# Last two output columns of a decoder layer: their tokens split 384 + 136 instead of 256 + 264

## The chip, the cores and the metric

The kernel runs on one core of one Trainium2 chip. The metric is the device time of one execution in microseconds (us); lower is better. A core has TensorE (PE, matmuls; its weight loads are shown apart as PEld), VectorE (DVE), ScalarE (ACT), GpSimd (POOL) and SyncE (SP), which run their own instruction streams and wait for each other by semaphores, and 16 DMA engines. A queue issues a DMA from the instruction stream of SP or ACT.

## What is computed

One layer of a hybrid decoder on 512 prompt tokens and 8 sample tokens (520 together), model width 2048, all in f32:

```python
h = h + jnp.concatenate([o, pool_out], axis=-1) @ w_out
gate, up = jnp.split(rmsnorm(h, g_ffn) @ w_gate_up, 2, axis=-1)
h = h + (jax.nn.silu(gate) * up) @ w_down
h = h + jax.nn.sigmoid(rmsnorm(h, g_ple) @ w_ple_gate) * (p_i @ w_ple_proj)
...
y_prompt = rmsnorm(hp, g_final)
y_sample = rmsnorm(hs, g_final)
```

The change lies in the last two lines' stage: the gated per-layer embedding (the fourth line) and the final norm, whose result `y_prompt` (512 x 2048) is 4.2 MB and `y_sample` (8 x 2048) 64 KB.

## The kernel before

Activations are kept transposed: a tile is 128 model columns (partitions) by T = 520 tokens, and h is 16 such tiles (KD = 16, P = 128). Each f32 product is made of three matmuls in rounded f32 (`float32r`): weights and activations are split into a high and a low part, and high x high, high x low and low x high are summed in PSUM. ScalarE makes the high part of the weights (L1378), VectorE the low part (L1932). Every matmul has its own load of 128 x 128 weights.

In the last stage a column tile m of the output needs 16 x 3 matmuls over the model width for the gate (accumulator `acc`), and 2 x 3 for the projection of the embedding (`scores`). Then VectorE multiplies the gate's sum by the row's inverse root (`gate_row`), ScalarE takes the sigmoid, VectorE multiplies by the projection and adds to h, ScalarE writes h times the final gain (`hg_row`) and h squared, GpSimd adds up the squares over the tiles, TensorE turns the scaled tile into rows of tokens (one transposition for each block of 128 tokens, into `mail_bank`, and one for the 8 sample tokens, into `o_bank`), and ScalarE copies the rows back over h. In tiles 0 to 13 all 520 tokens go together, as two matmuls of 260 columns each.

The last two tiles, 14 and 15, are split by tokens, so that a part of the tokens is complete before the matmuls end. `quarter(i)` gives for i = 0 to 3 the tile (s = 0, 1), the part of the tokens (a = 0, 1), its slice and its length: quarters 0 and 1 are the first 256 tokens of tiles 14 and 15, quarters 2 and 3 the remaining 264. TensorE runs for each quarter `half_column` (24 matmuls), the turn of the quarter before (`half_turn`, L1331), 12 matmuls, for i = 2 and 3 the row sums of the squares (`row_sums`, L1342: a matmul of 128 x 128 squares with a column of ones for each block), the last 12 matmuls and six of the projection. A turn waits until ScalarE has written the scaled copy (`hg_ready`).

When the row sums of a part are there (`fin_stats`), `finish(a)` runs on ScalarE (L1902) and VectorE (L2605): ScalarE takes the roots (after a table load), VectorE the reciprocals, and then they scale the finished rows, 8 tiles (half of a block of 128 rows, 512 KB) at a time. ScalarE scales block 2a and stores each half itself (L1914, L1916); VectorE scales block 2a + 1 (L2615), and SP stores it when `y_scaled` says so (L706). The instructions of an engine run in the order of the code: on ScalarE and VectorE it is `half_column(0)`, `half_column(1)`, `finish(0)`, `half_column(2)`, `half_column(3)`, `finish(1)`. So the first half's stores are issued while TensorE works on quarters 2 and 3. The sample rows (`ys_nat`) are scaled and stored at the very end (L2617, L708). SP finally waits for all nine stores of y.

Of the kernel before, what the change touches and what calls it, by code (L numbers as in the profile page):

```python
# [20 lines left out]
ALU = mybir.AluOpType  # L21
ACT = mybir.ActivationFunctionType
# [6 lines left out]
P = 128  # L29
D = 2048  # L30
SEQ = 512
NB = 8
T = SEQ + NB
# [21 lines left out]
HK = KD // 2  # L55
# [158 lines left out]
def quarter(i):  # L214

    s, a = i % 2, i // 2
    return s, a, (slice(0, 2 * P), slice(2 * P, T))[a], (2 * P, T - 2 * P)[a]


def is_first(i):  # L220
# [9 lines left out]
def layer(nc, x_prompt, x_sample, p_prompt, p_sample, cache_k, cache_v, state_pool, page_table,  # L230
# [17 lines left out]
    with ExitStack() as ctx:  # L248
# [3 lines left out]
        def ps(name, shape):  # L252
            return ctx.enter_context(nc.psum_tensor(name, shape, F32))

        def sem(name):
            return ctx.enter_context(nc.semaphore(name))
# [42 lines left out]
        sum_sq = sums[:, 0:T]  # L299
        sq = [sums[:, (2 + i) * T:(3 + i) * T] for i in range(2)]  # L300
# [8 lines left out]
        h_all = late.rearrange("p (k t) -> p k t", k=KD)  # L309
# [65 lines left out]
        fin = region[:, 8 * T + D:8 * T + D + 16]  # L375
# [45 lines left out]
        acc = [ps(f"acc{i}", [P, 2, 512]) for i in range(2)]  # L421
        sc = ps("scores", [P, 2, 512])
        mbank = ps("mail_bank", [P, 512])
# [3 lines left out]
        def out(t):  # L427
            return acc[t % 2][:, :, 0:HT]

        fin_sums = [acc[0][:, 0, 320:321], acc[0][:, 0, 321:322], acc[1][:, 0, 320:321], sc[:, 0, 320:321],  # L430
                    acc[0][0:NB, 0, 322:323]]
        bank_x = [acc[0][:, 0, 0:HT], acc[1][:, 0, 0:HT]]
        bank_y = [acc[0][:, 1, 0:HT], acc[1][:, 1, 0:HT]]
        bank_z = [sc[:, 0, 0:HT], sc[:, 1, 0:HT]]
# [16 lines left out]
        S = {n: sem(n) for n in names}  # L451
# [12 lines left out]
        def y_rows(b, k):  # L464

            return y_prompt[0, b * P:(b + 1) * P, :].rearrange("p (k n) -> p k n", n=P)[:, k:k + HK, :]

        def y_cells(b, k):

            return h_all[:, k:k + HK, b * P:(b + 1) * P]  # L470
# [7 lines left out]
        def _(sp):  # L478
            def load(slab, src, first=False):

                if not first:
                    sp.wait_ge(S["w_low_done"], slab.index - 1)
                k = src.shape[1]
                sp.dma_start(raw[slab.slot][:, :].rearrange("p (k n) -> p k n", k=k), src)\
                    .then_inc(raw_landed[slab.slot], 16)
# [215 lines left out]
            load_wp(KD // 2 - 1)  # L701
            for m in (KD - 2, KD - 1):
                load(Slab(PLE_N + m), w_pg_v[:, :, m * P:(m + 1) * P])
            for n, (b, k) in enumerate(((1, 0), (1, HK), (3, 0), (3, HK))):
                sp.wait_ge(S["y_scaled"], n + 1)
                sp.dma_start(y_rows(b, k), y_cells(b, k)).then_inc(S["y_stored"], 16)  # L706
            sp.wait_ge(S["y_scaled"], 5)
# [8 lines left out]
        def _(pe):  # L716
# [11 lines left out]
            def begin(slab, t, first=False):  # L728
                pe.wait_ge(S["w_low_done"], slab.index + 1)
                if not first:  # L730
                    pe.wait_ge(S["acc_free"], t - 1)
# [599 lines left out]
            def half_turn(i):  # L1331

                s, a, tokens, n = quarter(i)
                pe.wait_ge(S["hg_ready"], KD - 2 + i + 1)
                pe.wait_ge(S["y_taken"], KD - 2 + i)
                for b in (2 * a, 2 * a + 1):
                    ins = pe.transpose(mbank[:, b * P:(b + 1) * P], hg_row[s][:, b * P:(b + 1) * P], ident)
                if a:
                    ins = pe.transpose(obank[0:NB, 0:P], hg_row[s][:, SEQ:T], ident)
                ins.then_inc(S["y_turned"], 1)  # L1340

            def row_sums(squares, blocks, start, stop):  # L1342

                def add(out, rows):
                    return pe.matmul(out, rows, ones[:, 0:1], start=start, stop=stop, skip_group_check=True)
                for b in blocks:
                    ins = add(fin_sums[b], squares[:, b * P:min((b + 1) * P, T)])
                return ins

            for i in range(4):  # L1350
                if i < 2:
                    begin(Slab(PLE_N + KD - 2 + i), PLE_T + KD - 2 + i)
                half_column(i, range(HK))
                if i == 0:
                    turn_y(KD - 3, 1)
                else:
                    half_turn(i - 1)
                half_column(i, range(HK, HK + 4))
                if i == 2:
                    pe.wait_ge(S["pool_summed"], KD * 2 + KD)  # L1360
                    row_sums(sum_sq, (0, 1), True, True).then_inc(S["fin_stats"], 1)
                elif i == 3:
                    pe.wait_ge(S["pool_summed"], KD * 2 + KD + 1)
                    row_sums(sum_sq, (2, 3, 4), True, False)
                half_column(i, range(HK + 4, KD)).then_inc(S["acc_ready"], 1)
                half_projection(i)
            half_turn(3)
            pe.wait_ge(S["squared"], KD * 2 + KD + 2)
            row_sums(sq[1], (2, 3, 4), False, True).then_inc(S["fin_stats"], 1)

        @block.scalar
        def _(act):
            A = Steps(act, S["act_step"])
# [50 lines left out]
            for k in range(KD):  # L1424
                c, b = divmod(k, 4)
# [453 lines left out]
            def half_column(i):  # L1879

                s, a, tokens, n = quarter(i)
                m, done = KD - 2 + s, KD - 2 + i + 1
                tile = h_all[:, m, tokens]
                act.wait_ge(S["acc_free"], PLE_T + done)
                act.activation(silu_row[s][:, tokens], gate_row[s][:, tokens], ACT.Sigmoid).then_inc(S["silued"], 1)
                if i == 3:
                    act.activation(fin[:, 7:8], eps, ACT.Sqrt, scale=1.0 / D, bias=eps)
                act.wait_ge(S["pool_summed"], KD * 2 + m - 1)
                act.wait_ge(S["h_done"], done)
                act.activation(hg_row[s][:, tokens], tile, ACT.Copy,  # L1890
                               scale=gains[:, m + V_FINAL:m + V_FINAL + 1]).then_inc(S["hg_ready"], 1)
                act.activation(sq[s][:, tokens], tile, ACT.Square).then_inc(S["squared"], 1)
                if i == 1:
                    act.activation(fin[:, 5:6], eps, ACT.Sqrt, scale=1.0 / D, bias=eps)
                act.wait_ge(S["squared"], KD * 2 + done)
                act.wait_ge(S["y_turned"], done)
                if a:
                    act.activation(ys_nat[:, m * P:(m + 1) * P], obank[0:NB, 0:P], ACT.Copy)
                act.activation(h_all[:, m, a * 2 * P:(a + 1) * 2 * P], mbank[:, a * 2 * P:(a + 1) * 2 * P],
                               ACT.Copy).then_inc(S["y_taken"], 1)  # L1900

            def finish(a):  # L1902

                act.wait_ge(S["fin_stats"], a + 1)
                for b in ((0, 1), (2, 3, 4))[a]:
                    n = NB if b == 4 else P
                    act.activation(fin[0:n, b:b + 1], fin_sums[b], ACT.Sqrt, scale=1.0 / D,
                                   bias=eps[0:n, :]).then_inc(S["fin_root"], 1)
                if not a:
                    act.activation(fin[:, 6:7], eps, ACT.Sigmoid)  # L1910
                act.wait_ge(S["fin_inv"], 2 * a + 1)
                act.wait_ge(S["y_taken"], KD + 2 * a)
                for k in (0, HK):
                    A.step(act.activation(y_cells(2 * a, k), y_cells(2 * a, k), ACT.Copy, scale=fin[:, 8 + 2 * a:9 + 2 * a]))  # L1914
                    A.wait()
                    act.dma_start(y_rows(2 * a, k), y_cells(2 * a, k)).then_inc(S["y_stored"], 16)  # L1916
            half_column(0)
            half_column(1)
            finish(0)
# [5 lines left out]
        def _(dve):  # L1925
            V = Steps(dve, S["dve_step"])
            tt, stt, ts = dve.tensor_tensor, dve.scalar_tensor_tensor, dve.tensor_scalar
# [615 lines left out]
            for v in range(ND):  # L2543
                n, q = NS + v, len(resident(v // 4)[1])
# [59 lines left out]

            def finish(a):  # L2605

                dve.wait_ge(S["fin_root"], 2 + 3 * a)
                dve.reciprocal(fin[:, 8 + 2 * a:10 + 2 * a], fin[:, 2 * a:2 * a + 2]).then_inc(S["fin_inv"], 1)
                if a:
                    dve.reciprocal(fin[0:NB, 12:13], fin[0:NB, 4:5]).then_inc(S["fin_inv"], 1)  # L2610
                dve.wait_ge(S["fin_inv"], 2 * a + 1)
                dve.wait_ge(S["y_taken"], KD + 2 * a)
                for k in (0, HK):
                    cells_b = y_cells(2 * a + 1, k)
                    ts(cells_b, cells_b, fin[:, 9 + 2 * a:10 + 2 * a], None, ALU.mult).then_inc(S["y_scaled"], 1)  # L2615
                if a:
                    ts(ys_nat, ys_nat, fin[0:NB, 12:13], None, ALU.mult).then_inc(S["y_scaled"], 1)  # L2617
            half_column(0)
# [72 lines left out]
```

## Time and profile before

| | us |
|---|---|
| median of 3 runs | 2339.3 (2337.1 to 2341.42) |
| the profiled execution, device time | 2344.21 |
| its span in the trace | 2342.4 |
| TensorE busy in the span | 2270.8 (97%) |
| VectorE busy | 1639.2 (70%) |
| ScalarE busy | 1080.8 (46%) |
| GpSimd busy | 191.8 (8%) |
| mean granted clock of TensorE | 0.99 |

The page of a profile shows how busy each engine was, 40 slices of the span, the DMA queues, the chain of work that ended last (followed back from the last instruction to whatever released it), and groups of instructions. Times on the trace's axis start at the span's begin; the split tiles lie between 2296.9 and its end. A busy TensorE isn't TensorE at its peak, and the trace gives matmuls a modelled end: the pace is read from the starts of many, as in the chain, and not from the mean of one. An engine's idle time costs only if it is on the chain.

### The profile page before, as it was taken

The numbers are of one execution on the slowest core, as the hardware profiler recorded it, in microseconds if no ns is written. First come the engines' busy times: TensorE is split into PE (matmuls) and PEld (weight loads), VectorE is DVE, ScalarE is ACT, GpSimd is POOL, SyncE is SP. The second block draws the span as 40 slices with busy tenths as digits, with TensorE's granted clock in tenths as the row PEclk, the third lists the DMA queues.
The fourth block names the chain that finished last, engine by engine and source line by source line (L and its number), as shares of the span: only waits on it lengthen the run. The fifth ranks groups of instructions, "written<-read, shape, count | busy, mean of one in ns | idle before, by whom it ended". The sixth has DMA issues, their size and how long they took to land.

```text
span 2342.4 us, 45807 instructions
## 1 busy us (share of the span) xinstructions
PE 2270.8 (97%) x18549; PEld 2219.8 (95%) x18549; DVE 1639.2 (70%) x2125; ACT 1080.8 (46%) x1639; POOL 191.8 (8%) x88
## 2 busy tenths in 40 slices
PE   7999999999999999999999999999899999989997
PEld 6988898888999999999999999999899999979997
DVE  5355555564257888888888888888777777885333
ACT  5334444443245455454445454554434444564434
POOL 0041112301221000000000000000000000121111
PEclk9999999999999999999999999999999999999999
DMA  7454565543334445454554545457966865532332
GB/s 251 141 167 155 163 195 179 175 122 128 93 90 150 119 134 171 139 171 139 161 149 136 160 132 161 136 171 224 299 178 191 235 179 148 148 90 82 88 107 80
DMA packets 488018, 359.44 MB, mean 153 GB/s; under 512 B 8417, under 2 KB 469298, under 8 KB 487001
## 3 DMA queue, kind: packets, MB, share of 16 engines
q1 hardware_dynamic: 474921, 347.31, 50.2%
q10 hardware_dynamic: 13000, 10.78, 1.4%
q8 instruction: 67, 1.10, 0.2%
q14 instruction: 30, 0.25, 0.0%
HBM read 301.23 MB, written 57.29 MB: 153 GB/s over the span
## 4 chain that ended last, share of the span: by engine, by line
PE 91%; DVE 4%; DMA 2%; ACT 2%; issue 1%; SPq 0%; ACTq 0%; DVEq 0%
PE acc L1161 39%; PE acc L718 30%; PE scores L1161 15%; PE scores L718 2%; PE mail_bank L718 1%; PE o_bank L718 1%; DMA x_low<-act_low_rows 1%; DVE w_low L2378 1%; DVE w_low L1932 1%; DMA region<-in_x_prompt 1%; PE mail_bank L882 0%; DVE raw L2382 0%; ACT w_high L1378 0%; DVE x_low L1940 0%; DMA raw<-in_w_ple_gate 0%
## 5 line engine op out<-in xcount | busy, mean ns | idle before, releaser
L1161 PE MATMUL acc<-x_high,w_high 128*128 128x260 f32 x1584 | 449.2, 284 | 9.0 <-DMA x_low<-act_low_rows 6.4
L718 PE MATMUL acc<-x_high,w_high 128*128 128x260 f32 (+2 forms) x2048 | 437.4, 291 | 11.0 <-DVE w_low L1932 6.3
L1161 PE MATMUL acc<-x_low,w_high 128*128 128x260 f32 x1584 | 448.0, 283 | 0.0
L1161 PE MATMUL acc<-x_high,w_low 128*128 128x260 f32 x1584 | 447.7, 283 | 0.0
L718 PE MATMUL acc<-x_high,w_low 128*128 128x260 f32 (+2 forms) x2048 | 421.8, 284 | 0.0
L718 PE MATMUL acc<-x_low,w_high 128*128 128x260 f32 (+2 forms) x2048 | 421.5, 284 | 0.0
L2378 DVE TENSOR_TENSOR w_low<-raw,w_high 128x1024 fp32r<-128x1024 f32 (+4 forms) x252 | 285.6, 1134 | 121.3 <-ACT w_high L1704 120.3
L718 PEld LDWEIGHTS acc<-x_high,w_high 128*128 128x128 f32 x2048 | 320.4, 190 | 33.8 <-issue 24.2
L2378 DVE TENSOR_TENSOR w_low<-key_pages,w_high 128x1024 fp32r<-128x1024 f32 (+4 forms) x252 | 283.5, 1132 | 89.0 <-ACT w_high L1704 88.0
L718 PEld LDWEIGHTS acc<-x_low,w_high 128*128 128x128 f32 x2048 | 321.0, 190 | 0.1
L718 PEld LDWEIGHTS acc<-x_high,w_low 128*128 128x128 f32 x2048 | 321.0, 190 | 0.0
L1704 ACT ACTIVATE w_high<-key_pages 128x1024 fp32r<-128x1024 f32 (+4 forms) x252 | 244.4, 984 | 142.3 <-PE acc L1161 62.7
L1161 PEld LDWEIGHTS acc<-x_high,w_high 128*128 128x128 f32 x1584 | 299.2, 189 | 10.2 <-issue 7.4
L1161 PE MATMUL acc<-half_sums_high,w_high 128*128 128x260 f32 x1056 | 300.2, 284 | 5.0 <-DVE w_low L2378 3.0
L1704 ACT ACTIVATE w_high<-raw 128x1024 fp32r<-128x1024 f32 (+4 forms) x252 | 244.5, 984 | 120.8 <-PE acc L1161 58.4
L1161 PEld LDWEIGHTS acc<-x_low,w_high 128*128 128x128 f32 x1584 | 299.7, 189 | 0.0
L1161 PEld LDWEIGHTS acc<-x_high,w_low 128*128 128x128 f32 x1584 | 299.6, 189 | 0.0
L1161 PE MATMUL acc<-half_sums_low,w_high 128*128 128x260 f32 x1056 | 299.4, 283 | 0.0
L1161 PE MATMUL acc<-half_sums_high,w_low 128*128 128x260 f32 x1056 | 298.8, 283 | 0.0
L1707 ACT ACTIVATE sums<-acc 128x260 f32<-128x260 f32 x216 | 83.1, 385 | 322.6 <-PE acc L1161 321.7
L1161 PEld LDWEIGHTS acc<-half_sums_high,w_high 128*128 128x128 f32 x1056 | 198.9, 188 | 6.8 <-DVE w_low L2378 3.8
L1161 PEld LDWEIGHTS acc<-half_sums_high,w_low 128*128 128x128 f32 x1056 | 199.7, 189 | 0.0
(313 smaller groups left out, 4015.9 us busy)
## 6 DMA issues: line engine op xcount, KB each, us to landing
raw<-in_w_gate_up SPq DMA_DIRECT2D x44, 1024.0 KB, 6.8
key_pages<-in_w_gate_up SPq DMA_DIRECT2D x44, 1024.0 KB, 7.6
raw<-in_w_in SPq DMA_DIRECT2D x32, 1024.0 KB, 7.1
act_high_rows<-late_rounded SPq DMA_DIRECT2D x22, 910.0 KB, 5.3
act_low_rows<-late_rounded SPq DMA_DIRECT2D x22, 910.0 KB, 7.0
key_pages<-in_cache_k SPq DMA_DIRECT2D x32, 512.0 KB, 5.9
late<-in_cache_v SPq DMA_DIRECT2D x32, 512.0 KB, 6.0
raw<-in_w_out SPq DMA_DIRECT2D x16, 1024.0 KB, 5.8
```

What stands on the lines that cost most here:

```text
L718: return pe.matmul(o, l, r, start=start, stop=stop)
L1161: return pe.matmul(bank, w, x, start=start and first, stop=last, skip_group_check=True)
L1704: act.activation(wh[PLACE[i] // 2][:, at:at + q * P], src[:, 0:q * P], ACT.Copy).then_inc(S["part_high"], 1)
L1707: act.activation(dest, src, ACT.Copy).then_inc(S["copied"], 1)
L1932: tt(wl[slab.home][:, 0:n * P], raw[slab.slot][:, 0:n * P], wh[slab.home][:, 0:n * P].bitcast(F32), ALU.subtract).then_inc(S["w_low_done"], 1)
L2378: tt(wl[PLACE[i] // 2][:, at:at + c], src[:, 0:c], wh[PLACE[i] // 2][:, at:at + c].bitcast(F32), ALU.subtract).then_inc(S["part_low"], 1)
```

## The change

The first part now has three blocks of tokens (384), the second one block and the sample tokens (136). Everything that counts blocks follows: the turns take 3 and 1 blocks (`PART_BLOCKS`), the row sums blocks 0 to 2 and then 3 and the samples; in the first `finish` ScalarE takes three roots and scales and stores three halves (both of block 0 and the first of block 2), VectorE three (both of block 1 and the second of block 2), and in the second `finish` each has one half of block 3. Row sums have other cells of PSUM. The number of matmuls over the model width and of stores is the same.

```diff
@@ quarter, L214 @@
-    return s, a, (slice(0, 2 * P), slice(2 * P, T))[a], (2 * P, T - 2 * P)[a]
+    return s, a, (slice(0, 3 * P), slice(3 * P, T))[a], (3 * P, T - 3 * P)[a]
+
+
+PART_BLOCKS = ((0, 1, 2), (3,))
@@ fin_sums, L430 @@
-        fin_sums = [acc[0][:, 0, 320:321], acc[0][:, 0, 321:322], acc[1][:, 0, 320:321], sc[:, 0, 320:321],
-                    acc[0][0:NB, 0, 322:323]]
+        fin_sums = [acc[0][:, 0, 400:401], acc[0][:, 0, 401:402], acc[0][:, 0, 402:403], sc[:, 0, 400:401],
+                    acc[1][0:NB, 0, 400:401]]
@@ sync, L704 @@
-            for n, (b, k) in enumerate(((1, 0), (1, HK), (3, 0), (3, HK))):
+            for n, (b, k) in enumerate(((1, 0), (1, HK), (2, HK), (3, HK))):
@@ tensor: half_turn and row sums @@
-                for b in (2 * a, 2 * a + 1):
+                for b in PART_BLOCKS[a]:
...
-                    row_sums(sum_sq, (0, 1), True, True).then_inc(S["fin_stats"], 1)
+                    row_sums(sum_sq, (0, 1, 2), True, True).then_inc(S["fin_stats"], 1)
...
-                    row_sums(sum_sq, (2, 3, 4), True, False)
+                    row_sums(sum_sq, (3, 4), True, False)
...
-            row_sums(sq[1], (2, 3, 4), False, True).then_inc(S["fin_stats"], 1)
+            row_sums(sq[1], (3, 4), False, True).then_inc(S["fin_stats"], 1)
@@ scalar: half_column and finish @@
-                act.activation(h_all[:, m, a * 2 * P:(a + 1) * 2 * P], mbank[:, a * 2 * P:(a + 1) * 2 * P],
-                               ACT.Copy).then_inc(S["y_taken"], 1)
+                rows = slice(a * 3 * P, SEQ if a else 3 * P)
+                act.activation(h_all[:, m, rows], mbank[:, rows], ACT.Copy).then_inc(S["y_taken"], 1)
...
-                for b in ((0, 1), (2, 3, 4))[a]:
+                for b in ((0, 1, 2), (3, 4))[a]:
...
-                for k in (0, HK):
-                    A.step(act.activation(y_cells(2 * a, k), y_cells(2 * a, k), ACT.Copy, scale=fin[:, 8 + 2 * a:9 + 2 * a]))
+                for b, k in (((0, 0), (0, HK), (2, 0)), ((3, 0),))[a]:
+                    A.step(act.activation(y_cells(b, k), y_cells(b, k), ACT.Copy, scale=fin[:, 8 + b:9 + b]))
                     A.wait()
-                    act.dma_start(y_rows(2 * a, k), y_cells(2 * a, k)).then_inc(S["y_stored"], 16)
+                    act.dma_start(y_rows(b, k), y_cells(b, k)).then_inc(S["y_stored"], 16)
@@ vector: finish @@
-                dve.wait_ge(S["fin_root"], 2 + 3 * a)
-                dve.reciprocal(fin[:, 8 + 2 * a:10 + 2 * a], fin[:, 2 * a:2 * a + 2]).then_inc(S["fin_inv"], 1)
+                dve.wait_ge(S["fin_root"], 3 + 2 * a)
+                blocks = slice(3, 4) if a else slice(0, 3)
+                dve.reciprocal(fin[:, 8:12][:, blocks], fin[:, 0:4][:, blocks]).then_inc(S["fin_inv"], 1)
...
-                for k in (0, HK):
-                    cells_b = y_cells(2 * a + 1, k)
-                    ts(cells_b, cells_b, fin[:, 9 + 2 * a:10 + 2 * a], None, ALU.mult).then_inc(S["y_scaled"], 1)
+                for b, k in (((1, 0), (1, HK), (2, HK)), ((3, HK),))[a]:
+                    ts(y_cells(b, k), y_cells(b, k), fin[:, 8 + b:9 + b], None, ALU.mult).then_inc(S["y_scaled"], 1)
```

The instructions of ScalarE from the row sums of the first part to quarter 2 (L1907 is a root, L1914 a scaling, L1916 its store, L1885 the sigmoid of a quarter), before:

```order
L1907 ACTIVATE region<-acc,constants 128x1 x2
L1910 ACT_TABLE_LOAD
L1910 ACTIVATE region<-constants 128x1
L1914 ACTIVATE late<-late,region 128x8x128
L1916 DMA out<-late 128x8x128
L1914 ACTIVATE late<-late,region 128x8x128
L1916 DMA out<-late 128x8x128
L1885 ACTIVATE region<-region 128x264
```

and after, with lines numbered three higher:

```order
L1910 ACTIVATE region<-acc,constants 128x1 x3
L1913 ACT_TABLE_LOAD
L1913 ACTIVATE region<-constants 128x1
L1917 ACTIVATE late<-late,region 128x8x128
L1919 DMA out<-late 128x8x128
L1917 ACTIVATE late<-late,region 128x8x128
L1919 DMA out<-late 128x8x128
L1917 ACTIVATE late<-late,region 128x8x128
L1919 DMA out<-late 128x8x128
L1888 ACTIVATE region<-region 128x136
```

One scaling and one store more stand ahead of the sigmoid of quarter 2. The same engine at the end of the program, from the last copies of turned rows on (L1898, L1899; then the roots, for which `scores` and `acc` hold the row sums), before:

```order
L1898 ACTIVATE region<-o_bank 8x128
L1899 ACTIVATE late<-mail_bank 128x256
L1907 ACTIVATE region<-acc,constants 128x1
L1907 ACTIVATE region<-scores,constants 128x1
L1907 ACTIVATE region<-acc,constants 8x1
L1914 ACTIVATE late<-late,region 128x8x128
L1916 DMA out<-late 128x8x128
L1914 ACTIVATE late<-late,region 128x8x128
L1916 DMA out<-late 128x8x128
```

and after:

```order
L1901 ACTIVATE region<-o_bank 8x128
L1903 ACTIVATE late<-mail_bank 128x128
L1910 ACTIVATE region<-scores,constants 128x1
L1910 ACTIVATE region<-acc,constants 8x1
L1917 ACTIVATE late<-late,region 128x8x128
L1919 DMA out<-late 128x8x128
```

One root, one scaling and one store are gone there. TensorE in the middle of quarter 3, around the turn of quarter 2 (L1337, L1339) that waits for ScalarE's scaled copy, before:

```order
L718 MATMUL acc<-x_low,w_high 128x264
L718 MATMUL acc<-x_high,w_low 128x264
L1337 MATMUL mail_bank<-constants,region 128x128 x2
L1339 MATMUL o_bank<-constants,region 8x128
L718 MATMUL acc<-x_high,w_high 128x264
```

and after:

```order
L721 MATMUL acc<-x_low,w_high 128x136
L721 MATMUL acc<-x_high,w_low 128x136
L1340 MATMUL mail_bank<-constants,region 128x128
L1342 MATMUL o_bank<-constants,region 8x128
L721 MATMUL acc<-x_high,w_high 128x136
```

The order is the same; a turn has one block instead of two, and the matmuls around it have 136 columns instead of 264.

## Rows read from the trace of the kernel before

**Rows 1.** The page, the chain that ended last: shares of the span by engine.

```profile
PE 91%; DVE 4%; DMA 2%; ACT 2%; issue 1%; SPq 0%; ACTq 0%; DVEq 0%
```

**Rows 2.** The chain from 2296 us on: start us, us, what, how many.

```profile
2296.89 2.84 PE acc L718 x24
...
2310.41 2.91 PE acc L718 x24
2313.32 0.22 PE mail_bank L1337 x2
...
2314.99 0.35 PE acc L1345 x4
...
2315.79 1.28 ACT L1910
...
2320.44 0.43 ACT region L1885
...
2322.53 0.44 PE mail_bank L1337 x2
...
2326.68 0.44 DVE region L2598
...
2331.54 1.16 ACT late L1914
```

**Rows 3.** ScalarE's timeline of the first finish; last, TensorE's waits, total, times, longest.

```profile
2317.20 1.14 ACT L1914 ACTIVATE late<-late,region 128x1024 f32<-128x1024 f32 x1
...
2318.81 1.15 ACT L1914 ACTIVATE late<-late,region 128x1024 f32<-128x1024 f32 x1 [0.48 <-ACT late L1914]
...
2320.44 0.42 ACT L1885 ACTIVATE region<-region 128x264 f32<-128x264 f32 x1 [0.48 <-ACT late L1914]
...
PE mail_bank L1337 <- ACT region L1890: 4.3, 2, 2.3
```

**Rows 4.** Weight loads by shape: busy us, mean ns of one; last, timeline of four loads.

```profile
L718 PEld LDWEIGHTS acc<-x_high,w_low 128*128 128x128 f32 x2048 | 321.0, 190 | 0.0
...
L1345 PEld LDWEIGHTS acc<-constants,sums 128*128 128x128 f32 x8 | 1.1, 189 | 0.1
...
L1289 PEld LDWEIGHTS o_bank<-constants,region 128*8 128x8 f32 x14 | 1.2, 87 | 0.0
...
2314.71 0.53 PEld L1345 LDWEIGHTS acc<-constants,sums 128*128 128x128 f32 x4
```

**Rows 5.** Matmuls by shape, plain f32 of few columns: busy us, mean ns of one.

```profile
L718 PE MATMUL mail_bank<-constants,late 128*128 128x2 f32 x128 | 14.7, 246 | 0.0
...
L718 PE MATMUL o_bank<-v_nat,small 128*128 128x128 f32 x96 | 14.1, 283 | 0.0
```

**Rows 6.** Operations of 520 and 264 columns, grouped by shape: busy us, mean ns.

```profile
L1859 ACT ACTIVATE region<-region 128x520 f32<-128x520 f32 x1 | 0.6, 637 | 5.6 <-DVE region L2579 5.6
...
L2598 DVE TENSOR_TENSOR region<-acc,rstd 128x264 f32<-128x264 f32 x2 | 0.9, 430 | 4.8 <-PE acc L718 4.8
...
L2579 DVE TENSOR_TENSOR region<-acc,rstd 128x520 f32<-128x520 f32 x1 | 0.7, 699 | 8.0 <-PE acc L718 8.0
```

**Rows 7.** Windows: engines' busy us (instructions), then granted clock, DMA share, GB/s.

```profile
156.00:160.00 4.00, 0.42 (x4) 0.21 (x2) 3.97 (x6) 0.00 (x0) 0.92 (x1) 1.00 0.41 128
...
161.00:164.00 3.00, 3.00 (x16) 3.00 (x15) 0.79 (x3) 1.29 (x6) 0.74 (x1) 0.50 0.93 343
...
553.00:557.00 4.00, 0.97 (x6) 0.75 (x4) 0.69 (x5) 3.58 (x12) 0.00 (x0) 1.00 0.01 2
557.00:563.00 6.00, 5.31 (x17) 4.53 (x18) 3.02 (x6) 2.32 (x6) 0.00 (x0) 0.50 0.84 313
...
2322.00:2324.00 2.00, 1.47 (x13) 1.45 (x14) 0.00 (x0) 1.32 (x4) 0.75 (x1) 1.00 1.04 302
```

**Rows 8.** DMA from 2330 to 2343 us: rate in 40 slices of 0.325 us, sum.

```profile
GB/s 0 0 0 0 0 0 0 0 0 8 265 254 328 230 323 298 301 295 238 326 299 299 301 304 302 298 414 203 175 184 274 233 173 175 136 19 0 0 0 0
DMA packets 4176, 2.16 MB, mean 166 GB/s; under 512 B 72, under 2 KB 4168, under 8 KB 4168
```

## The prediction

> **What bounds the kernel now.** I read the chain that ended last first: 91% of the span is TensorE [rows 1], so every microsecond of matmul counts until the stage's own end. Then the same chain over the last 47 us, where the whole change lies [rows 2]. The reader is to see four stretches there. Up to 2315.36 the chain is TensorE alone: quarter 0 of the split (column tile 14, tokens 0 to 255) begins at 2296.89 and takes 24 matmuls in 2.84 us for each half of its K sum, 0.118 us a matmul; quarters with 264 tokens take 2.91 us for 24, 0.121 us. From 2315.36 to 2322.53 it is ScalarE: the first `finish` (roots, a table load of 1.28 us, two scalings and two stores), after which comes the sigmoid of quarter 2, and only then what TensorE needs for `half_turn(2)`. TensorE runs out of work at about 2320.7 and stands still; its two waits for ScalarE's L1890 add up to 4.3 us, the other of them is at the very end [rows 3]. From 2322.53 to 2326.68 it is TensorE again, and from there to 2331.54 the chain of short operations that ends in the last scalings. From 2331.54 to the span's end at 2342.4, 10.86 us, the program scales and stores 2.16 MB [rows 8].
>
> **Wide quarters.** Quarters 0 and 1 grow from 256 to 384 tokens. No row has a rounded-f32 matmul of 384 columns; the step from 256 to 264 columns costs 0.003 us for 8 [rows 2], 0.41 ns a column, which is 2.4 GHz. So 384 columns take 0.118 + 128 x 0.00041 = 0.171 us. Each quarter has 48 + 6 matmuls: 108 x 0.0533 = **+5.8 us**, all on the path. Each turn gets a third block, 0.11 us each [rows 2]: +0.2 us. Slabs, low parts and the `acc_free` waits are ready long before; these cost nothing.
>
> **Narrow quarters.** Here is where I choose. If 136 columns cost what the slope says, a matmul takes 0.121 - 128 x 0.00041 = 0.069 us, and the wide quarters' loss is given back. But every matmul has its own load of 128 x 128 weights. A load of 8 columns lasts 87 ns and one of 128 lasts 190 ns, for rounded and plain f32 alike: 103 ns for 120 columns [rows 4]. The row sums, whose matmuls have one column and can't hold anything up, show loads spaced (0.53 - 0.19)/3 = 0.113 us [rows 4], and 128 matmuls of two columns kept TensorE busy 14.7 us, 0.115 us each [rows 5]. Those are plain f32, but the load is the same row. I take **0.114 us**: almost nothing is gained by making a matmul narrower than about 245 columns. The bounds are 0.069 us (the slope) and 0.147 us (a plain f32 matmul of 128 columns [rows 5]); 0.114 is nearest to the rows that have the same load.
>
> **To the first sums.** Quarter 2 has 36 matmuls ahead of its row sums: 36 x (0.114 - 0.121) = -0.25 us. The row sums take three blocks for two, two more records of 0.09 us: +0.2 us. They also wait for the squares of quarter 1. Before, the chain passes from the matmuls to the sums with no wait between [rows 2], and the two operations each on ScalarE and VectorE that lead to the squares grow by some 0.5 us at the slopes of [rows 3, 6]; GpSimd's addition grows too, by an amount that I don't know. TensorE gets there 0.15 us earlier after quarter 1's accumulator, with its six projection matmuls 0.3 us longer. I count 0, with +1 us as the bound. Sum at `fin_stats`: 5.8 + 0.2 - 0.25 + 0.2 = **+5.9 us** (2321.3 on the old axis).
>
> **ScalarE's first finish.** It now scales and stores three half blocks for two. One scaling and its store take 2318.81 - 2317.20 = 1.61 us [rows 3]; a third root takes 0.15 us. Queued behind on the same engine is quarter 2's sigmoid, on that VectorE's product, ScalarE's scaled copy, and `half_turn(2)` on TensorE. All of it is on the path: **+1.8 us**. VectorE's three scalings (0.7 us each) end long before the sigmoid. The pieces after the sigmoid are narrower. ScalarE gains (0.637 - 0.422)/256 = 0.84 ns a column, VectorE (0.699 - 0.430)/256 = 1.05 ns [rows 3, 6]; two operations on each with 128 columns fewer give -0.5 us. TensorE resumes at 2322.53 + 5.9 + 1.8 - 0.5 = 2329.7, +7.2 us. It ran out of work 42 narrow matmuls after the sums, 42 x 0.114 = 4.8 us, at 2326.1: the stall grows from 1.8 to **3.6 us**.
>
> **From the resumption to the last scalings.** One block fewer to turn (-0.11), 24 matmuls at -0.007 (-0.16), two records of row sums fewer (-0.2): -0.45 us. Then, up to the scalings, gate, sigmoid and scaled copy are narrower (-0.35), one block fewer is turned and copied (-0.2), one root fewer (-0.15): -0.7 us; VectorE's product and sum lie under the table load there and give nothing. The last scalings begin 7.2 - 0.45 - 0.7 = **+6.05 us** later.
>
> **The stores at the end.** Only block 3 and the sample rows are left, 1.11 MB for 2.16. At full rate the engines moved about 300 GB/s and at the end some 180 [rows 8]; the last part, with the sample rows, stays. 1.05 MB at 300 GB/s are 3.5 us, at the mean of 260 GB/s 4.0. I take **-3.7 us**. Issue doesn't bound it: ScalarE's last store leaves 1.6 us earlier after the scalings than before, with 0.5 MB still to move. The early stores, 3.1 MB, are issued up to 2328.1 and done by about 2335.5, ahead of the last ones (2338.3 and later).
>
> Sum at full clock: 6.05 - 3.7 = **+2.3 us**.
>
> **The clock.** The longer stall has a price of its own. TensorE's granted clock stayed at 1.00 through the present stall of 1.8 us [rows 7]. It fell to 0.50 (1.2 of 2.4 GHz) around both stalls of 3.6 us or so that the rows show: TensorE did nothing from 156.4 to 160.0, and from 161 to 164 it ran at 0.50; it stood from 554 to 557.7, and 557 to 563 are at 0.50 [rows 7]. The stage after the stall is 3.6 us of matmuls. With 3 us of them at half clock, if the loads slow down with it, some 1.5 us are lost, and a transposition or two more cost 0.1 each: **+1.6 us** (bounds 0 and 3.3, the whole stage at half clock). I take the fall as likelier than not, since a stall of this length never went by without one.
>
> Forecast: +3.9 us. The profiled execution would go from 2344.2 to 2348.1; the median of the runs, 2339.3, is 4.9 us below the profiled one, and I add to that: **2343.2 us**, 0.17% above. About 0.2%, 4.7 us, is the least that a measurement of this kernel tells from no change, so this is within it, and close to its edge.
>
> **Rivals.**
> (a) The clock holds through the stall: +2.3 us, 2341.6. For it: the stall of 1.8 us left it alone; against it: both of the longer ones.
> (b) Narrow matmuls follow their columns, 0.069 us. Then the sums are ready at most 0.6 us sooner than in my sum, since ScalarE's table load and copy of quarter 1 bound `finish` there; the stall ends by ScalarE as before; the last 24 give 24 x 0.045 = 1.1 us: +0.6 us at full clock, +1.6 with a fall, about 2340.4. For it speaks the slope of [rows 2], against it the spacing of the loads in [rows 4]. The Trainium skill, TensorE: Matmul & The Clock Gate, Back-to-back issue gap, gives columns divided by 2.4 GHz plus 2.5 ns for an isolated warm matmul, an estimate of 59 ns for 136 columns, which would come to this rival; no row here shows so narrow a matmul with a full load at that pace.
> (c) Slower: a rounded-f32 matmul this narrow loses its rate and costs what plain f32 does. One record at 0.15 us adds 36 x 0.036 = 1.3 us before the sums and 24 x 0.036 = 0.9 at the end: +6.1 us with the clock's fall, 2345.4. As two records of 0.147 us (0.29), TensorE and no longer ScalarE bounds the stretch after the sums: 6.3 + 3.9 + 4.2 more, +16.7 us, 2356. It decides from about 0.155 us a matmul even with the clock held. For it: the trace has no rounded matmul under 256 columns; against it: load and duration are otherwise alike.
> (d) The last stores are bound by latency rather than bytes, and 1.05 MB fewer save only 2 us: +5.6 us, 2344.9. Against it: the rate is near 300 GB/s for most of [rows 8].
> (e) The change does what it is meant to and more, since ScalarE's longer hold is hidden (the stores' issue overlapping the table load or the like) and the clock holds: -5 us or better. No row shows an 8 us error in my sum.
>
> **Chances.** Forecast 0.48 (its range 2341 to 2345.5); (a) 0.17, (b) 0.12, (c) 0.10, (d) 0.09, (e) 0.04. Slower by over 0.2% takes most of (c) and (d), and a third of the forecast's own case, which its bounds carry over the edge: 0.33. Faster: 0.05. Same: 0.62. The range reaches from (b) less the scatter of the runs to (c) in its milder form and the clock's upper bound: 2339.2 to 2348.
>
> **What would show each step.** 24 matmuls of quarter 0 in 4.1 us, and of quarter 2 in 2.75 us (1.65 under (b), 3.6 or more under (c)); the first `finish` on ScalarE 1.6 us longer, with three stores; TensorE's longest wait for L1893's copy some 3.6 us; a granted clock of 0.50 in the 3 us around the last 24 matmuls; 1.11 MB after the last scalings. I am wrong if the narrow matmuls are not near 0.114 us, or if the part after the last scaling shrinks by less than 3 or more than 4.5 us.

## The result

| | kernel before | changed kernel |
|---|---|---|
| median of 11 runs each, us | 2341.5 (2337.1 to 2346.1) | 2347.3 (2342.3 to 2348.5) |
| ratio, with its 95% interval | | 1.0023 (1.0016 to 1.0031) |
| span of the profiled execution, us | 2342.4 | 2343.5 |
| start of the first split matmul on its axis, us | 2296.9 | 2291.7 |
| from there to the end of the span, us | 45.5 | 51.85 |

By the ratio the changed kernel is slower by 0.23%, 5.4 us (3.7 to 7.3). The spans of the two profiled executions differ by 1.1 us only, since in the second the work ahead of the split tiles, which is the same program, happened to end 5.2 us earlier. So I compare from the start of the first split matmul: **the stage takes 6.3 us more**, and that agrees with the ratio. Every later figure "after the stage's start" is counted that way. A second profiled execution of the changed kernel (c_after, below) gave a span of 2346.8 us and a stage of 51.9.

The chain of the changed kernel, from the page:

```profile
PE 90%; DVE 5%; DMA 2%; ACT 2%; issue 1%; SPq 0%; ACTq 0%; DVEq 0%
```

Its end, the same view as [rows 2] (start us, us, what, how many; the lines of the changed kernel are numbered three higher):

```profile
2291.65 4.21 PE acc L721 x24
...
2311.46 2.63 PE acc L721 x24
2314.09 0.35 PE mail_bank L1340 x3
...
2315.74 0.62 PE acc L1348 x6
...
2322.79 1.11 ACTq L1919
...
2323.94 0.33 ACT region L1888
...
2325.55 0.47 PE mail_bank L1340
...
2326.24 2.46 PE acc L721 x12
...
2331.93 0.31 DVE region L2601
...
2336.32 0.75 DVE late L2618
```

A wide quarter takes 4.21 us for 24 matmuls, 0.175 us each, a narrow one 2.63 us, 0.110 us. The first root begins at 2316.38, 24.73 us after the stage's start against 18.47 before. TensorE resumes at 2325.55. Twelve matmuls that took 1.29 us before the stall take 2.46 us after it.

ScalarE's hold, the same view as [rows 3] (DMA_DIRECT2D is the issue of a store; the last line is TensorE's wait: total, times, longest):

```profile
2321.61 1.15 ACT L1917 ACTIVATE late<-late,region 128x1024 f32<-128x1024 f32 x1 [0.48 <-ACT late L1917]
2322.79 1.11 ACTq L1919 DMA_DIRECT2D out<-late  x1
2323.94 0.32 ACT L1888 ACTIVATE region<-region 128x136 f32<-128x136 f32 x1 [1.19 <-issue]
...
PE mail_bank L1340 <- ACT region L1893: 5.8, 2, 4.5
```

The third store's issue took 1.11 us where the first two took 0.40. TensorE stands still 4.5 us, from 2321.05 to 2325.55; in the kernel before it was 2.0 us (4.3 in two waits, less the one of 2.3 at the end [rows 3]).

The clock and the last stores, the same views as [rows 7] and [rows 8] (windows as there; rate in 40 slices of 0.35 us from 2330 us on, and its sum):

```profile
2316.00:2320.00 4.00, 4.00 (x38) 4.00 (x38) 2.46 (x5) 3.11 (x7) 0.00 (x0) 1.00 0.27 81
2326.00:2332.00 6.00, 6.00 (x32) 5.96 (x30) 0.07 (x1) 0.42 (x2) 0.25 (x1) 0.50 0.63 182
...
GB/s 0 0 0 0 0 0 0 0 0 0 0 0 0 0 0 0 0 0 0 0 0 0 16 268 278 322 301 299 299 303 301 306 389 103 0 0 0 0 0 0
DMA packets 2096, 1.11 MB, mean 80 GB/s; under 512 B 40, under 2 KB 2088, under 8 KB 2088
```

TensorE begins 38 groups of matmuls in 4 us at 1.00 and only 32 in 6 us at 0.50. The granted clock fell during the stall, at 2323.6, 2.6 us after TensorE had stopped. It wasn't back at 2333.2, after 7.6 us of work without a gap, nor later. The stores at the end do what they should: 1.11 MB instead of 2.16, and none of the slow tail of [rows 8].

Where the 6.3 us come from, in times after the stage's start:

| us | before | changed | difference |
|---|---|---|---|
| first root of the first finish | 18.47 | 24.73 | +6.26 |
| from it to the sigmoid of quarter 2 | 5.08 | 7.56 | +2.48 |
| from that until TensorE resumes | 2.09 | 1.61 | -0.48 |
| from there to quarter 3's gate | 4.15 | 6.38 | +2.23 |
| from there to the last scalings | 4.86 | 4.39 | -0.47 |
| from there to the end of the span | 10.86 | 7.18 | -3.68 |
| sum | 45.51 | 51.85 | +6.34 |

### The profile page after: what moved, and what is told of

The parts are those of the page before. It is cut to its first block, busy times and chain, and to the rows that moved or that the text cites. A ratio compares the mean times of both kernels' runs of the same rounds, so it can differ in the third digit from the quotient of the medians.

```text
span 2343.5 us, 45803 instructions
## 1 busy us (share of the span) xinstructions
PE 2277.2 (97%) x18547; PEld 2226.7 (95%) x18547; DVE 1637.8 (70%) x2125; ACT 1081.1 (46%) x1639; POOL 191.7 (8%) x88
## 4 chain that ended last, share of the span: by engine, by line
PE 90%; DVE 5%; DMA 2%; ACT 2%; issue 1%; SPq 0%; ACTq 0%; DVEq 0%
PE acc L1164 39%; PE acc L721 30%; PE scores L1164 15%; PE scores L721 2%; PE mail_bank L721 1%; PE o_bank L721 1%; DVE w_low L2381 1%; DMA x_low<-act_low_rows 1%; DVE w_low L1935 1%; DMA region<-in_x_prompt 1%; DVE x_low L1943 1%; PE mail_bank L885 0%; DVE raw L2385 0%; ACT w_high L1381 0%; DMA raw<-in_w_down 0%
```

## The experiments

The stage's time is one trace for each version; the two traces of the changed kernel agree within 0.03 us (51.85 and 51.88). Each ratio is to the kernel before in the same set of runs; where the intervals of two versions overlap, only the traces tell them apart. Of each edit the lines that carry it are shown.

My theory after this result: the split itself costs 6.3 us of TensorE, since a matmul can't be spaced closer than its weight load; ScalarE's hold makes a stall of 4.5 us; that stall costs half of the clock for the rest of the stage, some 3 us; and the stores give 3.7 us back. The main rivals: the clock falls because the matmuls are narrow, whatever the stall; or all of the loss is stall and clock and the split costs nothing.

**e1_act_two: the hold back to two stores.** ScalarE takes two halves, VectorE four:

```diff
-                for b, k in (((0, 0), (0, HK), (2, 0)), ((3, 0),))[a]:
+                for b, k in (((0, 0), (0, HK)), ((3, 0),))[a]:
...
-                for b, k in (((1, 0), (1, HK), (2, HK)), ((3, HK),))[a]:
+                for b, k in (((1, 0), (1, HK), (2, 0), (2, HK)), ((3, HK),))[a]:
```

> The changed kernel, but ScalarE scales and stores two halves in the first finish and VectorE four (SP stores those). Theory (ScalarE's third scaling and its store of 1.11 us hold back quarter 2, and the stall that follows costs the clock): ScalarE reaches the sigmoid of quarter 2 about 5.1 us after its first root instead of 7.6, TensorE stands still 2.0 us instead of 4.5, the clock stays at 1.00, and the stage from the first split matmul to the span's end (51.85 us changed, 45.5 before) takes about 46.3 us. Rival (the clock falls because the matmuls are narrow, whatever the stall): the stall is 2 us, but the matmuls after it are spaced 0.213 us, and the stage takes about 49.4 us. Rival (the third store of a queue is slow only with ScalarE's): SP's third and fourth stores are issued in 0.4 us each; if it goes by the queue they take about 1.0.

Measured: the sigmoid 5.24 us after the first root, a longest wait of 2.1 us, the stage 48.64 us for the 46.3 of the theory; ratio to the kernel before 1.0014 (1.0005 to 1.0024). So the hold was on the path: 2.3 us went with it. But the clock fell all the same, a microsecond after TensorE resumed at 2326.0 (windows; and, last, SP's third and fourth stores, start and duration of the two together):

```profile
2326.00:2327.00 1.00, 0.97 (x9) 0.95 (x10) 0.00 (x0) 0.61 (x3) 0.47 (x1) 1.00 1.07 309
2328.00:2332.00 4.00, 4.00 (x22) 3.96 (x21) 0.30 (x1) 0.16 (x1) 0.00 (x0) 0.50 1.03 301
...
2322.11 2.64 SPq L709 DMA_DIRECT2D out<-late  x2
```

The kernel before has about the same stall and kept its clock. My theory of the clock is too simple: the length of the stall alone doesn't decide. SP's third and fourth stores took 2.64 us to issue together, 1.08 and 1.56, where its first two took 0.4 each: the slow issue comes with the queue's third store within a few microseconds, not with ScalarE.

**e2_filler: the stall without idleness.** Ahead of `half_turn(2)`:

```diff
+                    if i == 3:
+                        for _ in range(34):
+                            mm(obank[:, P:P + HT], wh[0][:, 0:P], xh[:, 0, 0:HT])
```

> The changed kernel, with 34 more matmuls of 260 columns (4.1 us, into unused cells of o_bank) on TensorE ahead of half_turn(2), where it stands still 4.5 us. They compute nothing that is used. Theory (the idle stretch lowers the clock): clock 1.00 up to the last quarter's end, the matmuls of 136 columns after the stall at 0.111 us instead of 0.213, the stage 3.0 us shorter than changed, about 48.9 us, and the time about 0.12% under the changed kernel. Rival (narrow matmuls lose the clock by themselves): no change, or a fall a little later; the stage stays at 51 to 52 us.

Measured: TensorE resumes with the turn 33.9 us after the stage's start, as in the changed kernel; the stage takes 49.0 us, ratio 1.0014 (1.0004 to 1.0024).

```profile
2321.00:2328.00 7.00, 7.00 (x63) 7.00 (x61) 2.09 (x5) 4.16 (x6) 0.00 (x0) 1.00 0.89 251
2329.00:2332.00 3.00, 3.00 (x30) 2.96 (x29) 0.00 (x0) 0.42 (x2) 0.30 (x1) 1.00 1.04 301
```

The narrow matmuls after the filler keep the full clock, for 4 us; in e6_after_late, below, matmuls of 136 columns run from 2316.2 to 2329.2, 13 us with their turns and row sums, at 1.00 and without a gap. So they don't lose it by themselves; here the fall came only with the stall. This also prices the clock that was lost up to the last gate: 51.85 - 49.0 = **2.85 us**. It isn't quite all: in this kernel too the clock fell at 2333.8, while TensorE waited for its last turn, and that turn and the one of the samples took 0.71 us, as in the changed kernel, for 0.45 in e6_after_late at full clock. With that the half clock costs about 3.1 us.

**e3_split_only: the split, with the finishes of before.** Blocks 0 and 1 early, 2, 3 and the samples at the end, row sums, roots and reciprocals too:

```diff
-                for b, k in (((0, 0), (0, HK), (2, 0)), ((3, 0),))[a]:
+                for b, k in ((2 * a, 0), (2 * a, HK)):
...
-                for b, k in (((1, 0), (1, HK), (2, HK)), ((3, HK),))[a]:
+                for b, k in ((2 * a + 1, 0), (2 * a + 1, HK)):
```

> The changed kernel's split of the tokens (384 and 136), but the finishes in the groups of before: blocks 0 and 1 early, blocks 2, 3 and the samples at the end. Theory (the split itself costs what the wide quarters add, since a narrow matmul can't go below its weight load): first root 6.1 us later after the stage's start than before, ScalarE reaches the sigmoid 5.1 us after its first root, stall 2.0 us, clock 1.00, 10.9 us from the last scaling to the end; the stage takes 45.5 + 6.1 - 0.5 - 0.45 - 0.5 = 50.2 us. Rival (the split costs nothing at full clock, all of the loss is the stall and the clock): 46 us or less. If the clock falls in spite of a stall of 2 us, 53 us.

Measured: first root at 24.50, a longest wait of 2.0 us, the stage 52.9 us, ratio 1.0023 (1.0013 to 1.0032). That is the third of the cases that were expected, 53 us with the clock's fall: it fell here too, at 2325.3, after a stall of 2 us:

```profile
2323.00:2325.00 2.00, 0.20 (x3) 0.18 (x3) 0.60 (x2) 0.93 (x3) 0.00 (x0) 1.00 1.04 293
2326.00:2332.00 6.00, 6.00 (x32) 5.96 (x31) 0.30 (x1) 0.48 (x2) 0.00 (x0) 0.50 0.28 81
```

The split is the bulk of the loss: the first root is 6.0 us late by it alone, before any stall. The rival that it costs nothing falls.

**e4_before_held: a long stall with wide matmuls.** In the kernel before, ScalarE copies 2560 unused columns after its two early stores:

```diff
+                if not a:
+                    for at, n in ((2880, 1024), (2880, 1024), (2880, 512)):
+                        A.step(act.activation(flat[:, at:at + n], flat[:, at:at + n], ACT.Copy))
+                        A.wait()
```

> The kernel before, with ScalarE held 2.7 us longer after its two early stores by three copies of unused cells. Theory (a stall of 4.5 us costs the clock and the hold is on the path): sigmoid of quarter 2 2.7 us later, TensorE stands still 4.5 us instead of 1.8, the clock falls to 0.50 and the 264 columns after it are spaced 0.22 instead of 0.121 us, which costs up to 3 us more; the stage takes 45.5 + 2.7 + 2 to 3 = 50.2 to 51.2 us. Rival (only narrow matmuls keep the clock down): the clock comes back within the last quarter as it did after the earlier stalls, and the stage takes 48.2 to 49.8 us.

Measured: the sigmoid 2.85 us later, a longest wait of 4.8 us, the stage 50.0 us, ratio 1.0014 (1.0005 to 1.0024). At the border of the two expectations, and the trace says why: the clock fell at 2326.5, when TensorE was at work again, and came back within the same quarter, 3.4 us later.

```profile
2321.00:2326.00 5.00, 0.18 (x2) 0.00 (x0) 0.86 (x2) 3.73 (x6) 0.00 (x0) 1.00 0.93 267
2327.00:2329.00 2.00, 2.00 (x11) 2.00 (x11) 0.00 (x0) 0.18 (x1) 0.09 (x1) 0.50 0.00 0
2330.00:2332.00 2.00, 2.00 (x17) 2.00 (x18) 0.38 (x1) 0.00 (x0) 0.00 (x0) 1.00 0.00 0
```

After a stall as long as the changed kernel's, 264 columns brought the clock back in 3.4 us, and 136 columns not in 7.6, in both traces of the changed kernel. Wide matmuls aren't always so quick: at 541 us in the trace of e6_after_late those of 260 columns worked 6 us at 0.50 before it was back.

**e7_act_two_wide: narrow or early?** The kernel of e1_act_two, whose quarters 2 and 3 compute 264 columns (256 to 519) and use the last 136:

```diff
-                        ins = mm(acc[s][:, a, 0:n], w, x[:, k, tokens], start=k == 0 and c == 0, stop=k == KD - 1 and c == 2)
+                        ins = mm(acc[s][:, a, 0:n + a * P], w, x[:, k, (slice(0, 3 * P), slice(2 * P, T))[a]], start=k == 0 and c == 0, stop=k == KD - 1 and c == 2)
```

> The kernel of e1_act_two, with quarters 2 and 3 computing 264 columns over the model width, of which 128 are not used (the projection keeps 136). Theory (after a stall of 2 us the clock falls only where the matmuls are narrow): 96 matmuls at 0.121 instead of 0.111 us, of which those before the stall only shorten it, a stall of 1.6 us, the clock at 1.00 to the end of quarter 3, stage about 48.6 - 2.5 + 0.6 = 46.7 us. Rival (the fall depends on when the stall comes, not on the width): the clock falls after the stall as it did there and the stage takes 48.5 us or more.

Measured: the stage 47.2 us against 48.6 in e1_act_two, ratio 1.0006 (0.9996 to 1.0015).

```profile
2323.00:2325.00 2.00, 0.47 (x4) 0.26 (x3) 0.60 (x2) 0.69 (x3) 0.00 (x0) 1.00 1.02 279
2325.00:2329.00 4.00, 3.82 (x33) 3.76 (x33) 0.00 (x0) 0.75 (x4) 0.48 (x1) 1.00 1.04 300
```

With nearly the same stall the clock holds. **With 128 useless columns in each matmul the stage is 1.5 us shorter**, in one trace against one; the intervals of the two ratios overlap.

**e8_200_columns and e9_240_columns: where the width stops to count.** The same edit with 64 and 104 extra columns instead of 128.

> The kernel of e1_act_two with 200 columns in the matmuls over the model width of quarters 2 and 3 (64 of them not used). Theory (a matmul can't be spaced closer than its weight load, and above that goes by columns): 24 matmuls of quarter 2 take 2.63 us as with 136 columns, 0.111 us each from start to start. Rival (the cost rises from 136 to 264 columns in proportion): 0.116 us, 2.75 us. The clock after the stall of 2 us: open; it fell with 136 columns and held with 264.

> The same with 240 columns (104 of them not used). Theory (weight load as the floor, met where the columns' own time of 0.121 us at 264 less 0.41 ns a column comes down to it, at about 240): 24 matmuls in 2.65 to 2.70 us. Rival (in proportion): 2.84 us. The clock after the stall: open, more likely to hold than with 200.

The first 24 matmuls of quarter 2, in the chains of 200, then 240 columns:

```profile
2312.12 2.67 PE acc L721 x24
```

```profile
2313.76 2.69 PE acc L721 x24
```

136 columns take 2.63 us, 200 take 2.67, 240 take 2.69, and 264 take 2.91. Nothing is gained below about 240, and above that it goes by columns, as it must if the weight load is the floor. With 200 columns the clock fell after the stall (stage 48.7 us); with 240 it had already fallen in the stall, and came back 3 us after it (stage 48.05 us). Windows of 200, then 240 columns:

```profile
2325.00:2330.00 5.00, 5.00 (x27) 4.96 (x26) 0.30 (x1) 0.26 (x1) 0.00 (x0) 0.50 1.04 301
```

```profile
2326.00:2328.00 2.00, 2.00 (x12) 2.00 (x11) 0.00 (x0) 0.42 (x2) 0.25 (x1) 0.50 1.04 301
2329.00:2331.00 2.00, 2.00 (x19) 1.97 (x20) 0.30 (x1) 0.00 (x0) 0.00 (x0) 1.00 1.04 302
```

These two are single runs. With a stall of 2 us the clock fell 0.5 to 1.1 us after it with 136 and 200 columns (e1_act_two, e3_split_only, e8_200_columns), in its last moment with 240, and not at all with 264 (the kernel before, e7_act_two_wide).

That looks like a rule of the width, and it isn't shown to be one. The trace of the kernel before has falls with 260 columns at gaps that are shorter still, which I had overlooked. After 1.54 us without a matmul, up to 539.15, the clock fell at 539.9; in a gap of 1.70 us, from 750.1 on, it fell at 751.5:

```profile
540.00:543.00 3.00, 3.00 (x16) 3.00 (x15) 2.76 (x11) 0.00 (x0) 0.00 (x0) 0.50 1.03 293
750.00:751.00 1.00, 0.10 (x1) 0.00 (x0) 1.00 (x2) 0.41 (x1) 0.00 (x0) 1.00 1.14 480
752.00:753.00 1.00, 1.00 (x5) 1.00 (x6) 1.00 (x2) 0.59 (x1) 0.00 (x0) 0.50 0.91 389
```

The second gap is the same program in every version and 1.7 us long in all twelve traces. The clock fell in two of them (the kernel before and e4_before_held) and held in ten; the changed kernel's, from 752 on:

```profile
752.00:754.00 2.00, 2.00 (x16) 2.00 (x17) 2.00 (x3) 0.81 (x1) 0.00 (x0) 1.00 0.64 275
```

So neither the length of a short gap nor the width of the matmuls decides by itself whether the clock falls. What does, stays open, and that it held in e7_act_two_wide may be chance.

**e6_after_late: the changed kernel without its stall.** The stores of e1_act_two, with ScalarE's two scalings and their stores moved out of the first finish behind quarter 2's squares (`scale(0)`), and VectorE's two of block 2 behind its part of quarter 2:

```diff
                 act.activation(sq[s][:, tokens], tile, ACT.Square).then_inc(S["squared"], 1)
...
+                if i == 2:
+                    scale(0)
                 act.wait_ge(S["squared"], KD * 2 + done)
                 act.wait_ge(S["y_turned"], done)
```

> The changed kernel's split and early stores, with ScalarE scaling and storing two halves and VectorE's two of block 2 behind quarter 2's own work on both engines. Theory (the changed kernel lost by its stall of 4.5 us and 3 us of half clock, not by the split alone): no stall, clock 1.00 up to the end of quarter 3, first root 24.7 us after the stage's start as in the changed kernel, stage 44.1 us against 51.85 changed and 45.5 before; ratio about 0.9994 against the kernel before, and 0.6 us behind the same edit on the kernel before. Rival (narrow matmuls lose the clock even without a stall): 47 us.

**e5_before_late: ScalarE's part of that edit in the kernel before.**

> The kernel before, with ScalarE's two scalings and stores of the first part moved behind quarter 2's squares. Theory (the hold of ScalarE in the first finish makes the stall): TensorE doesn't stop at half_turn(2), the stage from the first split matmul to the end takes 45.5 - 2.1 = 43.4 us, ratio 0.999 against the kernel before. Rival (something else, a wait of VectorE or the early stores, then holds the last quarter or the last stores): 45 us or more.

Measured: e6_after_late 44.1 us for the stage, ratio 0.9994 (0.9985 to 1.0003); e5_before_late 43.3 us, ratio 0.9985 (0.9976 to 0.9994). Neither stalls at `half_turn(2)`, and the clock is 1.00 up to the last turn in both; each has one wait left, for the last turn. e6_after_late, then e5_before_late:

```profile
PE mail_bank L1340 <- ACT region L1893: 2.0, 1, 2.0
```

```profile
PE mail_bank L1337 <- ACT region L1890: 2.3, 1, 2.3
```

Both stages came out within 0.1 us of what was expected. e5_before_late is the one version that its interval puts ahead of the kernel before, by 0.15%, and it has the old split. The new split's disadvantage with all stalls gone is 44.1 - 43.3 = 0.8 us by the traces; by the runs' intervals the two can't be told apart.

**c_after: the changed kernel once more.**

> The changed kernel itself on the same chip, for its scatter from run to run. Theory: first root 24.7 us after the stage's start, ScalarE's third store issued in 1.1 us, a stall of 4.5 us, the granted clock at 0.50 from the stall to the end, stage 51.9 us; ratio 1.0023 to 1.0027. If the clock's fall in the first look was a chance one, the matmuls after the stall are at 0.111 us here and the stage takes 49 us.

Measured: ratio 1.0025 (1.0016 to 1.0034), stage 51.88 us, first root at 24.73, a wait of 4.4 us, the clock at 0.50 from 2327.1, in the stall, to the end. The fall and its lasting came a second time.

## Why the prediction was right, and where its sum was short

The forecast was +3.9 us, 2343.2, within 0.2% but close to the edge, with 0.33 for slower; measured were +5.4 us by the runs and +6.3 by the trace. The time, 2347.3, lies in the range near its upper end. Of the 4.1 us that it is above the forecast, 2.2 are none of the change: the kernel before had a median of 2341.5 in these runs and not 2339.3. Against the mark of 0.2% the estimate is just beyond it, 0.23%, and its interval, 0.16 to 0.31%, has the mark inside, so the runs don't decide between same and slower. Neither of the prediction's signs of being wrong came: the narrow matmuls are near 0.114 us, and the part after the last scaling shrank by 3.68. The mechanisms were the right ones; the sizes of three terms were too small.

- **Wide quarters, +5.8: 6.2.** The slope taken from 256 and 264 columns, 0.41 ns, is 0.45 ns up to 384; a matmul took 0.175 us, not 0.171.
- **Narrow quarters, 0.114 us: 0.110.** The choice of the weight load over the columns, the main one of the prediction, holds: rival (b) would have had 1.65 us for 24 matmuls, rival (c) 3.6 or more; measured 2.63. With the turns and row sums the first root came +6.26 us late for +5.9.
- **ScalarE's first finish, +1.8: 2.5.** A third scaling and a third root cost what was said; the third store's issue took 1.11 us and not 0.40. No queue of before had three of these stores at once, but its trace has slow issues: SP took 1.0 us in the median, and up to 3.1, to issue each of the 16 loads of the last gate's weights. I had taken the first stores' 0.40 for every store.
- **Narrower pieces, -0.5: -0.48.** Right. The stall came out as 4.5 us for 3.6: 0.7 of the 0.9 by the store's issue, 0.1 by the matmuls between the sums and the stall, which took 4.7 us for 4.8. The stall of before, given as 1.8 us, was 2.0.
- **The clock, +1.6: 2.85 up to the last gate, about 3.1 in all.** This is the term that was most too small. I took it that 3 us would be at half clock, as from 161 to 164 in [rows 7]; it stayed at 0.50 to the end, near the upper bound of 3.3. e2_filler prices it; e4_before_held shows a return after 3.4 us with 264 columns. That the clock would fall came out right, but the reason, the stall's length, was too simple: e1_act_two and e3_split_only lost it with a stall of 2 us, and the trace of before lost it at gaps of 1.5 and 1.7 us. So what was said for rival (a), that a stall of 1.8 us had left the clock alone, was weak from the start.
- **To the last scalings, -0.45 and -0.7 at full clock.** The first stretch takes 3.55 us for 4.15 in e2_filler, and the second 4.13 for 4.86 in e6_after_late, each at full clock there: -0.6 and -0.7.
- **The stores at the end, -3.7: -3.68.** Right; rival (d), that they save only 2 us, falls.

At full clock the terms are 6.26 + 2.48 - 0.48 - 0.60 - 0.73 - 3.68 = +3.25 us, for the +2.3 of the prediction; the clock's 3.1 make it 6.3. What the change was to give is there, 3.7 us of stores. It went into 6.3 us of matmuls ahead of it, and the 2.0 us more that ScalarE held TensorE and the 3.1 of the clock came on top.

## What to carry to other kernels

Before splitting a matmul's columns, read the spacing of its weight loads: a part that is narrower than a load lasts costs the whole load, and here a part under about 240 columns gained nothing. An engine that both finishes early results and feeds the next matmuls should feed first: moving two scalings behind the squares, without any new split, gave 2.2 us of the stage, more than the new split could give under any arrangement tried. A gap of two microseconds on TensorE may cost nothing or half the clock for what follows, and one trace doesn't tell which, so look at the granted clock in several. Filling the gap kept the clock here (e2_filler), and taking the gap away was better still (e6_after_late). If neither can be done, wide matmuls after it brought the clock back in 3 to 6 us, and those of 136 columns never did.

## What the runs showed of the hardware that I had not expected

- In an idle stretch of 4.5 us the clock went from 2.4 to 1.2 GHz (1.00 to 0.50), and back-to-back matmuls of 136 columns, at 0.213 us each, did not bring it back in 7.6 us; of 264 columns they did in 3.4 us (e4_before_held), and of 260 in 3 to 6 us elsewhere in the traces. The same narrow matmuls hold the full clock if they come without a gap: 9.6 us before the stall (78 of them), and 13 us in e6_after_late.
- The same gap of 1.7 us, at 750 us, lost the clock in two traces of twelve.
- A matmul of 136 columns costs 0.110 us at the full clock and 0.213 at half: the floor that the weight load sets doubles with it.
- The load's floor at full clock agrees with the Trainium skill (TensorE: Matmul & The Clock Gate, LDWEIGHTS), which gives columns divided by 1.2 GHz, an estimate of 107 ns for 128. The Trainium skill's formula for an isolated warm matmul (same page, Back-to-back issue gap), an estimate of 59 ns for 136 columns, isn't the pace here, where each matmul has its own load: 110 ns. The section itself says that the formula leaves the load out, and gives about 81 ns for 128 columns with one; this kernel's 110 ns at 136 are above that too.
- The third store of 512 KB on a queue within a few microseconds took 1.04 to 1.11 us to issue, on SP and ScalarE alike, and a fourth 1.54 to 1.56, for 0.4. What the queue waits for there, the runs don't show.
